# The input projection of a hybrid block as seven block products, in two halves of the tokens, in one stream with attention and mixers

## The reference

```
mod = silu(c) @ w_ada + b_ada;  shift, scale, gate = split(mod, 3)
h = rmsnorm(x, g_pre) * (1 + scale) + shift
p = h @ w_in                      # 1024 -> 8704 columns, in 15 parts
y_pool = pool_mixer(a_in) * silu(a_g)            # window means of 2, 4, 8, 16 tokens
y_hgrn = hgrn2_mixer(b_q, b_f, b_i) * silu(b_g)  # gated linear recurrence, 4 heads of 64
y_conv = short_conv(c_x, c_b, c_c) * silu(c_g)   # 3 taps
y_diff = diff_attention(d_q, d_k, d_v) * silu(d_g)  # causal, 4 heads, two softmax maps each
gates = sigmoid(m_g)                             # 4 x 1024 columns
merged = sum over the branches of gates[b] * (y_b @ w_merge[b])
x = x + gate * rmsnorm(merged @ w_out, g_post)
```

## Time and profile before

| | |
|---|---|
| median of 3 runs | 2643.63 us (2642.55 to 2646.17) |
| the profiled execution | 2641.52 us, its span 2639.7 us |
| mean granted TensorE clock | 0.965 |
| PE busy | 2416.5 us, 92% |
| DVE busy | 1244.3 us, 47% |
| ACT busy | 950.1 us, 36% |
| POOL busy | 606.9 us, 23% |
| DMA moved | 293.28 MB, 111 GB/s |

### The profile page before, as it was taken

The page is one execution under the profiler, slowest core; times in us unless marked ns, Lnnn a source line. Parts: engine busy times, 40 slices in busy tenths (PEclk is TensorE's granted clock), DMA queues, the critical chain, the costliest instruction groups (busy, mean ns, idle before and its releaser), DMA issues. The chain is left out here.

```text
span 2639.7 us, 33253 instructions
## 1 busy us (share of the span) xinstructions
PE 2416.5 (92%) x12324; PEld 2007.3 (76%) x12324; DVE 1244.3 (47%) x2075; ACT 950.1 (36%) x2057; POOL 606.9 (23%) x594
## 2 busy tenths in 40 slices
PE   2799997899999999999799999999999945889898
PEld 2688885788888888888588888888888834667676
DVE  6522210455555555553456555655665434354442
ACT  3311111455555555554233223322332242334342
POOL 2400000122112211221223113211321224353443
PEclk8899998999999999999899999999999977999999
DMA  6245322423233323221332323232323176486682
GB/s 242 93 152 136 104 84 69 109 86 94 87 90 95 92 83 96 85 75 46 100 105 83 99 88 102 87 102 88 100 89 96 63 212 143 139 219 160 170 211 68
DMA packets 301882, 293.28 MB, mean 111 GB/s; under 512 B 24353, under 2 KB 223137, under 8 KB 300705
## 3 DMA queue, kind: packets, MB, share of 16 engines
q1 hardware_dynamic: 301728, 291.25, 37.5%
HBM read 192.08 MB, written 99.09 MB: 110 GB/s over the span
## 5 line engine op out<-in xcount | busy, mean ns | idle before, releaser
L1455 PE MATMUL bankB<-h_hi,B_w_hi 128*128 128x512 f32 x1024 | 411.4, 402 | 10.8 <-DVE B_w_lo L1225 10.8
L1457 PE MATMUL bankB<-h_hi,B_w_lo 128*128 128x512 f32 x1024 | 400.9, 392 | 0.0
L1456 PE MATMUL bankB<-h_lo,B_w_hi 128*128 128x512 f32 x1024 | 400.7, 391 | 0.0
L688 POOL TENSOR_TENSOR C_prob<-C_prob,C_cf 128x512 f32<-128x512 f32 (+3 forms) x160 | 152.7, 982 | 974.8 <-DVE C_cf L752 970.6
L821 ACT ACTIVATE C_prob<-C_sc,C_negm 128x512 f32<-128x512 f32 (+3 forms) x320 | 196.6, 620 | 282.0 <-DVE C_negm L727 276.8
L727 DVE TENSOR_REDUCE C_negm<-C_sc 128x2 f32<-128x1024 f32 (+3 forms) x160 | 170.4, 1065 | 246.3 <-PE C_sc L894 191.6
L878 PE MATMUL C_gb<-h_hi,C_w_hi 128*128 128x512 f32 x640 | 265.3, 414 | 0.1
L880 PE MATMUL C_gb<-h_hi,C_w_lo 128*128 128x512 f32 x640 | 251.2, 393 | 0.0
L879 PE MATMUL C_gb<-h_lo,C_w_hi 128*128 128x512 f32 x640 | 249.8, 390 | 0.0
L1371 ACT ACTIVATE B_g_out<-bankB 128x512 f32<-128x512 f32 x128 | 75.7, 592 | 477.2 <-PE bankB L1457 477.2
L1455 PEld LDWEIGHTS bankB<-h_hi,B_w_hi 128*128 128x128 f32 x1024 | 193.1, 189 | 56.9 <-DVE B_w_lo L1225 11.1
(11 more groups left out here) (230 smaller groups left out, 4744.0 us busy)
## 6 DMA issues: line engine op xcount, KB each, us to landing
gT_scratch<-B_g_out SPq DMA_DIRECT2D x128, 256.0 KB, 2.4
D_gate<-gT_scratch SPq DMA_DIRECT2D x32, 1024.0 KB, 9.6
pT_scratch<-C_p_out SPq DMA_DIRECT2D x80, 256.0 KB, 2.6
C_qt<-qB_scratch SPq DMA_DIRECT2D x128, 128.0 KB, 2.9
B_w_stage<-in_w_in_dram SPq DMA_DIRECT2D x32, 512.0 KB, 3.9
C_w_stage<-in_w_in_dram SPq DMA_DIRECT2D x40, 256.0 KB, 3.1
p_out<-in_w_ada_dram SPq DMA_DIRECT2D x8, 1024.0 KB, 5.3
w_stage<-in_w_in_dram SPq DMA_DIRECT2D x8, 1024.0 KB, 5.9
```

What stands on the lines that cost most here:

```text
L688: tt(second, second, cf[i % 2][:, 1, p:p + 1].to_broadcast([P, width(n)]), ALU.mult).then_inc(scaled, 1)
L1455: mm(bank[g][:, :], w_hi[j][:, k, :], h_hi[:, k, cols], start=(k == 0), stop=False)
L1456: mm(bank[g][:, :], w_hi[j][:, k, :], h_lo[:, k, cols], start=False, stop=False)
L1457: last = mm(bank[g][:, :], w_lo[j][:, k, :], h_hi[:, k, cols], start=False, stop=(k == KD - 1))
```

## The change

Stages A, C and B become one function, `trunk`. Stage D stays as it is.

**Seven products.** The unit is now a pair of column tiles (256 columns) by half of the tokens (1024). Its matrices are cut into 2 x 2 blocks: w into four blocks of 512 rows by 128 columns, h into four of 512 rows by 512 tokens. A block product is 4 chunks x 3 = 12 matmuls of 128x512. The plain way needs eight block products, Winograd's form of Strassen's scheme seven. There are 34 pairs x 2 halves = 68 units, 476 products, 5712 matmuls. The seven operands on the side of h are built once per half (`h11`, `h21`, `t2`, ...) and kept in SBUF split (`h_hi[0..6]`, `h_lo[0..6]`); the four sums on the side of w are built for each unit by POOL; on the side of the result ACT copies five products out of PSUM, DVE adds two onto such copies, POOL adds one block onto another. The two `gb` banks, the running sums that stay in PSUM (start only in products 0, 1 and 3) and four output tiles `o[0..3]` carry this.

**Two halves.** The first 34 units take tokens 0 to 1023, the others 1024 to 2047. The operands of the second half are made while the first is multiplied, stored to HBM and loaded at slots 230 to 242. The attention has a first part (48 pieces) and a second (112), the mixers 8 blocks of 128 tokens in each half.

**One stream.** Every engine walks over 486 slots. In slot n PE does product n, ACT copies product n-1 out and splits the high part of w for product n+3, DVE adds product n-1 and takes the low part for n+3, POOL makes the sums of the next unit in positions 4, 5 and 6 of 7. Behind that the tables `ATTENTION` and `MIX_BASE` put the attention steps and the parts of the mixer blocks. A mixer block now reaches over 28 slots, and a new one begins every 12 slots. The scores have three PSUM banks of one map each, so the maxima are taken one map at a time.

```diff
+PAIR_COLS = (28, 30, 32, 34, 24, 20, 26, 22) + (4, 6, 8, 0, 2, 10, 12, 14, 16, 18) + tuple(range(36, 68, 2))
+PRODUCTS = PER * UNITS
+SLOTS = PRODUCTS + 10
+LEAD, RING = 3, 4
+ATTENTION = ((62, 44), (287, 70))
+MIX_BASE = [130 + 12 * i for i in range(8)] + [374 + 12 * i for i in range(8)]
+        for half, (at0, span) in enumerate(ATTENTION):
+            for s in range(att_steps[half]):
+                att_after.setdefault(at0 + s * span // att_steps[half], []).append((half, s))
...
+            operand = (h11, h21, t2, h11, h12, h22, h21)
...
+        def source(n):
+            u, j = divmod(n, PER)
+            return (w1[:, :, 0:P], w2[u % 2][:, :, 0:P], s2[:, :, :], w1[:, :, P:2 * P], s3[:, :, :],
+                    w2[u % 2][:, :, 0:P], w2[u % 2][:, :, P:2 * P])[j]
...
+            def sum_s3_s1(u):                       # POOL, position 4
+                tt(s3[:, :, :], w1[:, :, 0:P], w1[:, :, P:2 * P], ALU.subtract).then_inc(s_made, 1)
+                tt(w1[:, :, P:2 * P], w1[:, :, P:2 * P], w2[u % 2][:, :, P:2 * P], ALU.add).then_inc(s_made, 1)
+            def sum_s2(u):                          # POOL, position 5
+                tt(s2[:, :, :], w1[:, :, P:2 * P], w1[:, :, 0:P], ALU.subtract).then_inc(s_made, 1)
+            def sum_s4(u):                          # POOL, position 6
+                tt(w2[u % 2][:, :, 0:P], w2[u % 2][:, :, 0:P], s2[:, :, :], ALU.subtract).then_inc(s_made, 1)
+            def cross(u):                           # POOL, position 5, before sum_s2
+                pool.wait_ge(copied, 5 * u + 4)
+                tt(o[2][:, :], o[2][:, :], o[3][:, :], ALU.add).then_inc(crossed, 1)
...
+            def high(n):                            # ACT, 3 slots ahead
+                if n >= RING:
+                    act.wait_ge(product_done, n - RING + 1)
+                a(w_hi[n % RING][:, :, :], source(n), ACT.Copy).then_inc(whi, 1)
+            def copy_out(n):                        # ACT, positions 0, 2, 3, 4, 6
+                act.wait_ge(product_done, n + 1)
+                a(o[b][:, :], gb[n % 2][:, :], ACT.Copy).then_inc(copied, 1)
+            def low(n):                             # DVE, 3 slots ahead
+                dve.wait_ge(whi, n + 1)
+                tt(w_lo[n % RING][:, :, :], source(n), w_hi[n % RING][:, :, :].bitcast(F32), ALU.subtract).then_inc(wlo, 1)
+            def add_out(n):                         # DVE, positions 1 and 5
+                tt(o[b][:, :], gb[n % 2][:, :], o[b][:, :], ALU.add).then_inc(summed, 1)
...
+            def product(n):                         # PE
+                pe.wait_ge(wlo, n + 1)
+                bank_free(n)                        # copied or summed of product n - 2
+                to, fresh = gb[n % 2][:, :], j in (0, 1, 3)
+                for k in range(KH):
+                    mm(to, hi[:, k, :], h_hi[j][:, k, :], start=(fresh and k == 0), stop=False, skip_group_check=True)
+                    mm(to, hi[:, k, :], h_lo[j][:, k, :], start=False, stop=False, skip_group_check=True)
+                    last = mm(to, lo[:, k, :], h_hi[j][:, k, :], start=False, stop=(k == KH - 1), skip_group_check=True)
...
+                    for m in range(2):              # PE, scores: three banks of one map
+                        q = 2 * z + m
+                        if q >= 3:
+                            pe.wait_ge(exp_done, q - 2)
...
+            def decays_second(i):                   # POOL: half of what DVE did in L1317, L1319
+                tt(QX[:, 1, 0:NL - 1, :], X[:, 1, 0:NL - 1, :], q_s[i % 2][:, 1, :]..., ALU.mult).then_inc(prep1, 1)
+                tt(X[:, 1, 0:NL - 1, :], X[:, 1, 0:NL - 1, :], k_s[i % 2][:, 1, :]..., ALU.mult).then_inc(prep1, 1)
```

2653 lines of the change are left out of this document (1417 added, 1236 removed).

## The result

The changed kernel takes 2887.25 us (median of 4 runs, 2884.36 to 2888.84), the kernel before 2644.61 us on the same chip (2642.55 to 2646.17). The ratio is 1.0917, 95% interval [1.0898, 1.0936]: 9% slower. Predicted were 2568 us, 2440 to 2680, and faster with a chance of 0.79. Both are wrong.

What follows compares the result with a forecast made beforehand. The prediction took PE as the bound up to 2112 us, apart from the 93.6 us start. PE's work of 2410 us plus stalls of 75 and 80 gave a 2565 us span, plus 4 is 2569, rounded 2568; range 2440 to 2680.

Steps and rivals of the forecast that it cites:

- Products: Product matmuls on PE: 2.72 us a slot, 6528 matmuls become 5712, 184 us less.
- Start: Before and in the first unit: first product at about 65 us, unit ends at 95 us, bounds 85 and 110.
- Stalls in the attention: PE waits on ACT and DVE in 64 two-step slots, 67 us, plus 8 at block ends: 75 us, bounds 0 and 160.
- Stalls in the mixers: PE waits in mixer blocks: 46.6 us a block, 5.0 over PE's own, 80 us in all, bounds 0 and 190.
- PE meets DVE's bursts: 2 us: Mixer blocks: PE meets DVE's bursts and POOL's runs before sums for w, 2 us a block.
- Change of operands: Slots 230 to 242, loading the second half's operands: hidden but for operands 4 and 5, 5 us, bounds 0 and 20.
- Stage D: The last stage, not touched by the change: 528 us.
- PE's wait for `C_prob` and `C_at` 60 to 90 us: Sign in the attention: PE's wait on ACT would be 60 to 90 us.
- Blocks 46 to 47 us apart: Sign in the mixers: blocks come 46 to 47 us apart; 42 or 52 would mean the forecast is wrong.
- Double slots at 8.8 us: Sign in the attention: slots with two steps take 8.8 us; 7.6 or 10 would mean the forecast is wrong.
- B: Rival, slower: DVE and POOL become the bound in the mixers, 200 us there and 110 in double steps, 2724 us; chance 0.16.
- C: Rival, all over the stream: gaps of 1 to 3 us lower PE's clock to 0.97, 53 us, 2622 us; chance 0.05.

Runs made afterwards that it cites:

- e1: The changed kernel with attention and mixers left out of the stream, products, sums, copies, splits and stage D kept: 1992.1 us.
- e13: As e12, with the start's modulation made of 32 matmuls over 512 columns and 16 tiny ones in place of 256 one-column matmuls: 2635.4 us.
- e6: As e5, with a finished output block's transpose in the middle of the next product and DVE's gate product in the same step: 2803.1 us.
- e5: The changed kernel with the edits of e2 and e3, attention over 50 and 84 slots, units reordered, second part from slot 273: 2858.6 us.
- e4: The changed kernel with six zero-operand matmuls on PE between the two attention steps of each double slot: 2870.1 us.
- e2: The changed kernel with the second attention step of a double slot moved to the middle of the next product: 2799.2 us.
- e9: The edits of e6 and e7 together, with the attention's gate units first and its second part from slot 280 in 77 slots: 2683.2 us.
- e3: The changed kernel with a mixer block's four transposes on PE, and their copy on ACT, two slots later: 2833.9 us.
- e7: As e3, with nine parts of a mixer block moved one slot later and the gate sigmoid four: 2806.3 us.
- e14: As e12, with both decay products of the second level half made by DVE in place of POOL: 2653.2 us.
- e10: As e9, with ACT's gate sigmoid of a mixer block placed beside its other sigmoids: 2655.1 us.
- e16: As e15, with the four scalings of a mixer block made by ACT in place of DVE: 2610.5 us.
- e12: As e10, with value products seven steps behind the scores in place of six, and mixer transposes one slot later again: 2651.6 us.
- e11: As e10, with DVE's run of seven distances cut into two runs in neighbouring slots: 2656.7 us.
- e15: As e13, with the first half's unit order and the mixer transposes (behind product base+1) taken back: 2620.0 us.

## Why the prediction was wrong

The span came out 317.6 us over the sum. The terms that failed are the stalls: 75 us for the attention and 80 for the mixers, against 249 and 179 measured, which is 273 of the 317.6. The start is 36 more. By the prediction's own steps:

1. *Products* (2.72 us a slot, 184 us less): right. e1 shows 2.72 in 294 us without a gap, with POOL's sums and DVE's low parts beside them.
2. *Start* (first product 65, first unit 95; bounds 85 and 110): the first unit ended at 131, 36 us late and outside the bounds. 14 of them are a step that the sum did not have at all. I counted transfers and operand chains, and gave PE's 256 small matmuls nothing; they take 52 us, from 17.9 to 70.0, and the first product waits for their end. e13 shows it (first product at 63.5 us). The others are in the first unit, 52 us in place of 30. DVE's and POOL's sums of 128x1024 run side by side there:

```profile
L746 POOL TENSOR_TENSOR A_x_all<-A_x_all 128x1024 f32<-128x1024 f32 x2 | 6.7, 3360 | 6.6 <-ACT A_x_all L954 6.6
L1239 DVE TENSOR_TENSOR A_ada<-A_ada,A_x_all 128x1024 f32<-128x1024 f32 x2 | 6.6, 3358 | 0.0
L1226 DVE TENSOR_TENSOR A_ada<-A_x_all,A_ada 128x1024 f32<-128x1024 f32 x2 | 6.2, 3156 | 0.0
```

   3.2 to 3.4 us each, where I counted 1.3 for DVE and 2.4 for POOL. I had the slowdown for the mixers and did not use it here. No experiment changed this unit, so that part is read from the trace and not shown.
3. *Stalls in the attention* (75 us, bounds 0 and 160): 249. This is the largest miss. The mechanism was right and its size wrong: the term 1.05 us x 64 = 67 us came as about 205. In the trace a double slot takes 9.8 us on average over the 64. The sum had put 7.6 there (2.72, two steps of 338 / 178 = 1.9 us, 1.05 of waiting); the 8.8 that the prediction named as its sign holds for two pieces of full width and never stood in the sum. The slots with one step take 5.2 to 5.6 us, 46 us of stall in all where 8 were given. Three things are in it. First, in the timeline laid out by hand DVE did only the low part and the maxima; the real one also has the gate of an output block and its weights in front of the maxima, and begins late. Second, I said that a slot with one step is covered by the next product. It is not covered where a block of queries ends: the transpose of the output block waits for DVE in the same slot, and so do the first value products two blocks later. e6 gained 55 us over e5, nearly all of it in attention 1. Third, attention 2 starts before its mask is there, 15.6 us. And a part is the clock, which the sum left out: 113 us at half clock in these slots, by e4's rate 38 to 56 us (an estimate). e2, e6 and e9 together bring the two parts from 904 us in 116 slots to 268 + 533 us in 129 slots; 13 more slots of products are 35 us, so 138 us of stalls went. (e5, e6 and e9 also spread the steps over more slots; how much that gave alone was not measured.)
4. *Stalls in the mixers* (80 us, bounds 0 and 190): 179, within the bounds, but for another reason than the forecast gave. I charged 8.2 of DVE's 44.6 us a block to POOL and let 2 us be the meeting of bursts. In the trace DVE had 340 of 457 us, so it was not full, and it did less than the forecast's own count (eight blocks at 44.6 us and 12 further slots make 367). PE waited up to 7.9 us at a time for the last part of the block before, which DVE does in that same slot. "PE meets DVE's bursts: 2 us" is the step that failed. e3 and e7 show it (53 and 28 us by moving parts a slot or two). POOL has a share in that wait all the same: the gate product in `finish` takes 1958 ns on average here and 666 in e14, where POOL does less two-input work, the last one 969 and 547, some 1.7 us a block (an estimate from the two traces).
5. *Change of operands* (5 us): slots 237 to 243 hold the late products, and slots 227 to 287 take 12.6 us more than 60 x 2.72, transpositions of v included. With the 27.5 us over in slots 7 to 62 that is 40 for the 21 + 5 of the sum, 14 too many. *Stage D* (528): 524. Near.

What would have shown it, against what came: PE's wait for `C_prob` and `C_at` 60 to 90 us, came as 88 (65.6 + 22.8). That was right, and yet a third of the attention's stalls. Low parts at 0.85 to 1.0 us: 0.90 and 0.93 in the two mixer parts. DVE near 90% busy: 74 to 76%. Blocks 46 to 47 us apart: 50 to 57.6. Double slots at 8.8 us: 9.8, near the 10 that was to mean the forecast is wrong.

*The rivals.* B gave 310 us of stalls and 2724 us. The side was right, its mechanism was not that of the changed kernel: DVE and POOL were not the bound. They came closer to it in e10 to e16, when most waits for the same slot were gone (e12's wait moved to DVE's additions; DVE busy for 89% of the mixers, PE for 93%), but no run shows them as the bound: e11 and e14 changed nothing, and e16's gain is not clear of noise. The two engines do hold each other up (e14). But that is at most a small part of the miss: in slots 119 to 227 of e1 the low parts were as slow (a mean of 945 ns) and no slot was late. The rule of the Trainium skill (page "SBUF — State Buffer", section "SBUF: two separate sides"), by which the prediction's sum would have been 40 us higher, agrees with e14 in direction; by itself it would have left the sum 278 us short, and it says nothing of the waits that made the loss. C (the clock, 53 us) was told as an alternative; it comes on top, and larger. From the first product to stage D the trace has 276 us at half clock, and by e4's rate of a third to a half that is 92 to 138 us, an estimate. Most of it goes when the waits go (99 us at half clock in e15).

*The chances.* 0.17 for slower was too low. The bounds of steps 3 and 4 alone reached 350 us over the sum without stalls, 2760; the range was cut to 2680. And the terms that I put at zero or near it (PE's small matmuls, single-step slots, the wait for a block's end) could only be wrong upwards.

## What to carry to other kernels

When several chains are interleaved by slots, let each instruction of PE need what others did in an earlier slot. Go through every wait of PE and ask in which slot its releaser stands and what stands before it on that engine; a wait for the same slot cost up to 8 us each time, with no engine full. One slot of distance can still be too little where the other engine runs late, and more distance can cost elsewhere (e12). Cover does not follow from an engine's busy share: a second step right behind the first had none, and in the middle of the next product it got 88 us back. When units are reordered, look at which function ACT does between two others: the edit that took the sigmoids out from among the logarithms and exponentials gained 92 us, and another such edit 28.
